# Products of a zero block on TensorE between the steps of the second batch's linear attention and attention

## The reference

```
h = rmsnorm(x) ; z = h @ w_in                       # one projection for both mixers
o_gla = gated linear attention, 4 heads (keys of 64, values of 128), in chunks with a carried state
o_fox = softmax(q k^T * scale + c[t] - c[s], s <= t) @ v, 8 heads of 64, c = cumulated log forget gates
x = x + concat(norm(o_gla) * silu(g), o_fox) @ w_out
PEER: q = rmsnorm(x) @ w_q; for each of 8 heads the 16 best of 128 x 128 product keys;
      x = x + sum over 8 * 16 experts of softmax(score) * gelu(u[idx] . h) * v[idx]
```

## Time and profile before

| | |
|---|---|
| time, 3 runs | 3239.22, 3239.26, 3245.87 us; median 3239.26 |
| the profiled execution | 3243.7 us, of which the span from first to last instruction 3241.8 us |
| TensorE matmul / VectorE / ScalarE / GpSimd busy | 2700.1 / 2478.3 / 1511.4 / 1307.6 us (83, 76, 47, 40%) |
| DMA | 1269.70 MB, mean 392 GB/s |
| mean granted TensorE clock | 0.926 |
| chain of waits that ended last | DMA 9%, PE 8%, DVE 2%, issue 2% |

### The profile page before, as it was taken

One profiled execution on the slowest core, in us unless ns is written; L12 is line 12 of the kernel. 1 busy time (PEld: TensorE's weight loads), 2 busy tenths in 40 slices (PEclk: granted clock), 3 DMA queues, 4 the chain that ended last, 5 costly groups with the idle time before them and its releaser, 6 DMA issues. The chain is left out here.

```text
span 3241.8 us, 32377 instructions
## 1 busy us (share of the span) xinstructions
PE 2700.1 (83%) x8464; PEld 1378.1 (43%) x8464; DVE 2478.3 (76%) x5460; ACT 1511.4 (47%) x3966; POOL 1307.6 (40%) x1062
## 2 busy tenths in 40 slices
PE   8878688887987898888978898888988898888766
PEld 4633354443433445443434444543433454444322
DVE  3597886998668768997678777998678776888864
ACT  2352553544235744454255654554246563444532
POOL 0134343343444444343443443444444434444443
PEclk9989759998999999998998999999999999999999
DMA  7499898999999999999999899999999999999998
GB/s 272 173 395 422 327 339 337 414 420 403 404 421 420 416 384 395 420 410 399 421 415 392 356 415 393 420 418 410 422 411 395 416 360 415 415 421 420 412 421 344
DMA packets 184561, 1269.70 MB, mean 392 GB/s; under 512 B 23368, under 2 KB 26840, under 8 KB 33336
## 3 DMA queue, kind: packets, MB, share of 16 engines
q0 software_dynamic: 152064, 1107.36, 83.8%
q1 hardware_dynamic: 29336, 150.37, 11.4%
q10 hardware_dynamic: 2976, 9.89, 0.8%
HBM read 1258.55 MB, written 9.00 MB: 391 GB/s over the span
## 5 line engine op out<-in xcount | busy, mean ns | idle before, releaser
L768 POOL DMA_INDIRECT uv_ring<-in_peer_uv,expert_index x1056 | 1302.7, 1234 | 1911.5 <-PE ps_acc L1348 1496.8
L1348 PE MATMUL ps_acc<-uv_ring,coef_diag 128*128 128x512 f32 x2920 | 1484.0, 650 | 417.7 <-ACT coef_diag L1028 397.3
L1713 DVE CUSTOM_DVE_ANT_0 uv_ring<-uv_ring,h_rows 128x1024 f32<-128x1024 f32 x1056 | 1281.8, 1220 | 401.3 <-DMA uv_ring<-in_peer_uv,expert_index 395.9
L1348 PEld LDWEIGHTS ps_acc<-uv_ring,coef_diag 128*128 128x128 f32 x2920 | 570.6, 205 | 1131.6 <-issue 567.8
L1023 ACT ACTIVATE gelu_u_dot_h<-u_dot_h 128x2 f32<-128x2 f32 x528 | 108.0, 205 | 1323.4 <-DVE u_dot_h L1713 1317.3
L1727 DVE SCALAR_TENSOR_TENSOR v_sums<-uv_ring,coefficients,v_sums 128x1024 f32<-128x1024 f32 x318 | 408.0, 1283 | 50.4 <-ACT coefficients L1030 45.8
L1106 PE MATMUL ps_scores<-weight_chunk,rows_T 128*128 128x512 f32 x784 | 356.4, 601 | 11.5 <-DMA weight_chunk<-in_w_in_chunks 11.5
L1028 ACT ACTIVATE coef_diag<-coef_diag,gelu_u_dot_h 128x128 f32<-128x128 f32 x730 | 268.8, 398 | 16.2
L1305 PE MATMUL ps_turn<-rows_T,weight_chunk 128*128 128x256 f32 (+1 forms) x1280 | 266.9, 364 | 2.9 <-ACT rows_T L928 2.6
L1020 ACT ACTIVATE coef_diag<-packed_consts,expert_weight 128x128 f32<-128x128 f32 x730 | 262.6, 390 | 0.4
L1305 PEld LDWEIGHTS ps_turn<-rows_T,weight_chunk 128*128 128x128 f32 x1280 | 228.1, 195 | 55.4 <-issue 31.1
(11 more groups left out here) (195 smaller groups left out, 2241.3 us busy)
## 6 DMA issues: line engine op xcount, KB each, us to landing
weight_chunk<-in_w_in_chunks SPq DMA_DIRECT2D x50, 1024.0 KB
weight_chunk<-in_w_peer_q_and_subkeys SPq DMA_DIRECT2D x40, 1152.0 KB
uv_ring<-in_peer_uv,expert_index POOLq DMA_INDIRECT x1056
weight_chunk<-in_w_out_chunks SPq DMA_DIRECT2D x16, 1024.0 KB
uv_ring<-in_w_in_chunks SPq DMA_DIRECT2D x10, 1024.0 KB, 15.3
x_mid<-in_x_rows SPq DMA_DIRECT2D x9, 512.0 KB, 10.4
uv_ring<-in_w_out_chunks SPq DMA_DIRECT2D x4, 1024.0 KB, 14.2
mix_rows<-in_x_rows SPq DMA_DIRECT2D x8, 512.0 KB
```

Source lines behind the costliest of these rows:

```text
L768: pool.indirect_dma_start(out=ring[:, s % RING, :], out_offset=None, in_=dram["uv"], in_offset=bass.IndirectOffsetOnAxis(ap=idx[:, t % IDX ...
L1348: mm = pe.matmul(acc[:, c, :], diag[:, r, :], ring[:, r, D + c * 512:D + (c + 1) * 512], start=first, stop=False, skip_group_check=True)
L1713: dve.tensor_tensor_reduce(out=ring[:, s % RING, 0:D], in0=ring[:, s % RING, 0:D], in1=h2[:], scale=1.0, scalar=0.0, op0=ALU.mult, op1=ALU ...
```

## The change

TensorE gets a new helper, `add_zeros`, and calls it ahead of each step of `gla` (8 times) and of `attend` (4 times) when the batch is the second (`bi == 1`, tiles 1 and 2). Its weights are rows 64 to 127 and columns 0 to 63 of the first mask in `causal`, which are all zero; the moving operand is rows 64 to 127 of both masks, 256 bf16 columns. The product, 64 x 256 zeros, is added to a part of `acc` (`start=False`). The products have no semaphore, neither a wait nor an increment, and the other engines' programs stay as they are.

```
+        def add_zeros(count):
+
+            zeros, masks_ = causal[P // 2:P, 0, 0:P // 2], causal[P // 2:P].rearrange("p a t -> p (a t)")
+            for _ in range(count):
+                pe.matmul(acc[0:P // 2, 1, 0:2 * P], zeros, masks_, start=False, stop=False, skip_group_check=True)
...
             for g in range(gla_steps(t)):
                 if t == 0:
                     keep_busy(3)
+                if bi == 1:
+                    add_zeros(8)
...
             for n in range(att_steps(t)):
                 if t == 0:
                     keep_busy(1)
+                if bi == 1:
+                    add_zeros(4)
```

## The result

| | median, us | lowest to highest | runs |
|---|---|---|---|
| before | 3241.59 | 3232.12 to 3251.93 | 8 |
| after | 3254.03 | 3242.41 to 3265.11 | 8 |

The ratio is 1.0034, 95% interval 1.0021 to 1.0048: the change costs 7 to 16 us. The forecast was slower, 3293 us. The time lies in the range that was given, 3230 to 3312 us, but in the range of none of its cases, and the loss is a quarter of the one forecast. Single runs of either kernel differ by some 20 us, so that one profile shows the stages and only the ratio shows the total.

The account below looks back on a forecast made before the run. TensorE at its low clock was taken to bound attention: 336 products at 0.20 us, 67.2, less 3.6 at the high clock and 11.8 of waits, 51.8; with +2 for linear attention +54, on 3239.3 gives 3293 us, range 3230 to 3312.

Parts of the forecast that it names:

- its cases: Five outcomes for the whole kernel: 3293 us (3275 to 3312), 3267 (3255 to 3275), 3236 (3226 to 3242), 3345, 3239.
- what bounds the stages: Tiles 1 and 2: VectorE bounds linear attention (busy 68.72 of 72.50 us), TensorE at its low clock bounds attention.
- a forecast of +2: Linear attention, 224 products: mostly hidden in TensorE's 24.2 us of waits, +2 us, bounds -4 and +15.
- The price of a product: One added TensorE product: 0.109 us at the high clock, 0.20 us at the low one.
- it falls there or at the next stall and then stays down through both tiles: Likeliest case, attention of tiles 1 and 2: low clock throughout, 51.8 us there, 3293 us in total, chance 0.45.
- the fillers cover the wait of 2.38 us only partly: Start of attention, wait for copies of keys and queries: 16 products fill 1.7 us of 2.38 us.
- the forecast case: Low clock through the attention of both tiles: +54 us with linear attention, 3293 us (3275 to 3312), chance 0.45.
- Rival 3: Attention of tiles 1 and 2: fillers hold the high clock, about -5 us there, total -3, 3236 us; chance 0.27.
- heads of 2.86 and 3.46 us: Attention heads of tiles 1 and 2 at the high clock with twelve added products; 2.76 and 3.94 us before.
- Halving the turn and the sum: Attention heads: time outside the score taken as half at the high clock, 1.31 us halved in tile 1.
- the transposes and the first output products: Ends of the attention tiles at the high clock: transposes halved, about -2 us for both; first output products -1.5 us.

Follow-up runs that it names:

- e2: Kernel after without the zero products in attention, 8 a step kept in linear attention; ratio to the kernel before 1.0002, attention 70.1 us.
- e4: Kernel after with 2 zero products a step in both linear attention and attention; ratio to the kernel before 1.0111, attention 102.9 us.
- e7: Kernel after with none in linear attention and 4 a step of 32 rows in attention; ratio to the kernel before 1.0197, attention 133.3 us.
- e5: Kernel after with none in linear attention, 2 a step of 128 rows and 128 weight columns in attention; ratio to before 0.9986, attention 66.4 us.
- e3: Kernel after with none in linear attention, 4 a step in attention only from step 14 of tile 1 on; ratio to before 1.0182, attention 127.5 us.
- e8: Kernel after with none in linear attention, 12 ahead of every third attention step; ratio to the kernel before 1.0008, attention 72.1 us.
- e9: Kernel after, attention only: 128-row products, 2 a step, 1 in the heads' loop (steps 14 to 31); ratio to before 0.9968, attention 61.5 us.
- e1: Kernel after without the zero products in linear attention, 4 a step kept in attention; ratio to the kernel before 1.0027, attention 76.3 us.

## Why the prediction was right and wrong

The direction was right, and so was what bounds the stages: the attention carries the loss, and the linear attention hides most or all of its 224 products (e2's total is 1.0002; the +1.2 us of the profile against a forecast of +2 is within what that stage varies). The price of a product was right too. The timeline of the kernel after at the start of tile 1, with ScalarE's copy of the queries:

```profile
408.08 1.93 PE L1070 MATMUL ps_acc<-causal_neg 64*64 64x256 bf16 x16
409.04 0.58 ACT L877 ACTIVATE mixing_or_attention<-ps_turn 128x512 f32<-128x512 f32 x1
409.94 0.70 PE L1183 MATMUL ps_scores<-k_pairs_T,mixing_or_attention 64*128 64x256 f32 x2
410.57 0.28 PE L1184 MATMUL ps_scores<-neg_c_parts_rows,head_of_parts 96*128 96x256 bf16 x1
410.69 0.22 PE L1186 MATMUL ps_scores<-causal_neg,ident_b 128*128 128x128 bf16 x1
410.84 1.49 PE L1070 MATMUL ps_acc<-causal_neg 64*64 64x256 bf16 x12
```

Sixteen in a row are (1.93 - 0.27) / 15 = 0.111 us each at the high clock, for 0.109 forecast.

The step that failed is the choice of the case: "it falls there or at the next stall and then stays down through both tiles". The clock stayed at 1.00 from the first scores on. The fall was taken over from the earlier trace rows, with the sentence that the fillers cover the wait of 2.38 us only partly. They covered it: the copies that the scores need ended at 409.04 + 0.58 = 409.62 us and the 16 products at 409.94, with no idle time shown before the scores, and the 12 between each two scores and those up to the first turn closed the gap after them as well. I had set 1.7 us of products against 2.38 us as if the wait's length were fixed. It isn't. In the kernel before, the same copy is

```profile
409.40 0.58 ACT L877 ACTIVATE mixing_or_attention<-ps_turn 128x512 f32<-128x512 f32 x1
```

Counted from the dot product of slot 73 it ends 4.4 us on in both kernels (409.98 - 405.55 before, 409.62 - 405.26 after), behind the back's gelu and coefficients on ScalarE. The transposes that it copies began 1.1 us on before and 1.8 us on after, behind zero products of their own. So a part of the wait was taken up there already. Nor does an idle rest decide it: ahead of the first scores e4 left a wait of 0.82 us and fell, e7 left none and fell, e5 left 1.38 us and held. How many products stand at the first scores, and how full they are, is what these runs show to matter, and the rows of before had nothing on it. That the clock would stay down once it had fallen was right for half-row products, and e3 with +58 us in the attention and a ratio of 1.0182 is what the forecast case looks like. It needed the products to come after the fall.

Rival 3 then is what happened, and its sum had the wrong sign, -5 us for the attention where it was +6.6: heads of 2.86 and 3.46 us were forecast, 3.25 and 3.85 measured. Of the 0.39 us, 0.23 are the zero products (1.54 for 1.31: in groups of four and eight they take more than in a long row), and the rest is the work: 1.71 against 1.55. Halving the turn and the sum wasn't at fault: in e8, where the two stand side by side, the work takes 2.94 - 1.42 = 1.52 us. The term that I had at nothing is the change between work and half-row products, twice a head; e8 takes one of the two groups away and 0.31 of the 0.39 us with it. Why a change costs that stays open; in e5 the work beside full products takes 1.42. I also took the transposes and the first output products as -3.5 us at the ends; with no wait left, each tile's end carried its zero products in full instead. Between the tiles this shows: from tile 1's last score products to tile 2's first it was 441.96 - 426.57 = 15.39 us before and 446.60 - 430.14 = 16.46 after.

On the two rules of the Trainium skill, "TensorE: Matmul & The Clock Gate": the advice to keep TensorE continuously busy ("Why this matters for your kernels") would have given the right level for the change, but e3 (35.00 of 35.00 us at 0.50) and e7 (3.40 of 3.40 us busy as it fell) contradict it as a rule: what TensorE is busy with matters, and which level it starts from. On transposes ("PE-mode transpose") nothing here adds to the earlier trace rows; where zero products part them, 12 with half of the rows in e3 and 12 with a quarter in e7, the clock stayed at 0.50.

## What to carry to other kernels

Filler products on TensorE aren't a matter of the engine's busy share. Give them all rows and columns (e5, e9: half the number or less does nearly the same, and the work beside them is shorter; which of the two matters more wasn't parted), put many where the engine would wait and only as few in a dense loop as hold the clock, and in as few groups as possible; and look at the stage's waits afterwards: where TensorE has none left while VectorE waits for it, the stage is paying for its fillers. With half or fewer of the rows, too few is worse than none or too many, since a clock that has fallen isn't lifted by them and every product then costs about double (e4, e7). Where another engine paces the stage, leave them out.

## What the hardware did that I had not expected

- The same loop can run at either level: with 4 half-row products a step at 1.00 (e1, attention 76.3 us) or 0.53 (e3, 127.5 us), by whether the clock was up when they began.
- With 2 full-array products a step it came back by itself within the heads' loop, at 452.7 us of e5.
- Going from 64-row zero products to fp32 work and back costs about 0.3 us for each further group a head (2.94 against 3.25 us), at the high clock. Eight zero products at the low clock take 1.84 us, 0.23 each.
- At 0.96 in place of 0.76, a stage that VectorE paces took 39.2 us in place of 39.6.
